# GpSimd forms the remaining parts of the weights of retention keys, retention values and pool input

## What is computed

```python
def hybrid_mixer(h, w_in, ...):
    proj = h @ w_in
    (dn_qkv, dn_z, dn_b, dn_a, ret_q, ret_k, ret_v, ret_g, pool_u, gates) = jnp.split(proj, ...)
    qkv = jax.nn.silu(causal_depthwise_conv(dn_qkv, dn_conv)).astype(f32)
    q, k, v = ...                       # l2_normalize of q and k
    beta, g = ...                       # from dn_b and dn_a
    o_dn = gated_delta_rule(q, k, v, beta, g)      # a triangular solve in chunks
    o_pool = multiscale_pool(pool_u, pool_w, pool_scale)
    o_ret = chunkwise_retention(rotary(ret_q), rotary(ret_k), ret_v, log_gamma)
    ...
def second_block(x, ...):
    for l in range(DEPTH):
        h = rms_norm_2(x, mix_pre_norm[l])
        x = x + rms_norm_2(hybrid_mixer(h, ...), mix_post_norm[l])
        h = rms_norm_2(x, ffn_pre_norm[l])
        x = x + rms_norm_2(swiglu(h, ...), ffn_post_norm[l])
```

## Time and profile before

| | |
|---|---|
| median of three runs | 1751.71 us |
| the profiled execution | 1752.36 us |
| its span in the trace | 1750.5 us |
| mean granted TensorE clock | 0.947 of full speed |

### The profile page before, as it was taken

The page is one execution under the profiler, slowest core; times in us unless marked ns, Lnnn a source line. Parts: engine busy times, 40 slices in busy tenths (PEclk is TensorE's granted clock), DMA queues, the critical chain, the costliest instruction groups (busy, mean ns, idle before and its releaser), DMA issues.

```text
span 1750.5 us, 18733 instructions
## 1 busy us (share of the span) xinstructions
PE 1587.8 (91%) x7866; PEld 1193.0 (68%) x7866; DVE 921.3 (53%) x1131; ACT 464.6 (27%) x621; POOL 44.9 (3%) x39
## 2 busy tenths in 40 slices
PE   6999999999998798799888799979879998979997
PEld 3755654565564496688744799859668874469986
DVE  2436652235754339865363666563876537266653
ACT  1121320031230144233201333333514330034332
POOL 0001000001000000000000000000000000000000
PEclk9999899999989898999999899989989999989999
DMA  7343122444212353243323365544414342245653
GB/s 263 121 145 120 48 97 81 160 144 134 83 68 82 122 169 121 80 137 121 127 97 122 119 185 177 195 148 152 136 49 145 121 151 96 68 142 176 192 176 113
DMA packets 140066, 226.75 MB, mean 130 GB/s; under 512 B 7968, under 2 KB 55376, under 8 KB 139856
## 3 DMA queue, kind: packets, MB, share of 16 engines
q1 hardware_dynamic: 133136, 221.60, 38.4%
q10 hardware_dynamic: 6848, 3.97, 0.8%
HBM read 224.50 MB, written 1.05 MB: 129 GB/s over the span
## 4 chain that ended last, share of the span: by engine, by line
PE 74%; DVE 18%; issue 3%; ACT 2%; POOL 1%; DMA 1%; ACTq 0%; POOLq 0%; DVEq 0%; SPq 0%
PE gp L475 19%; PE gp L458 19%; PE gp L487 17%; PE gp L529 6%; DVE arena L1055 5%; PE mp L714 4%; DVE arena L1094 3%; PE gp L451 3%; DVE wt_rest L1061 2%; DVE arena L1462 2%; POOL rs_out L1667 1%; PE mp L620 1%; PE mp L431 1%; DVE hT L1055 1%; DVE arena L1255 1%
## 5 line engine op out<-in xcount | busy, mean ns | idle before, releaser
L458 PE MATMUL gp<-wt,hT 128*128 128x512 f32 x512 | 227.9, 601 | 0.0
L458 PE MATMUL gp<-wt,arena 128*128 128x512 f32 x416 | 188.8, 614 | 22.2 <-DVE arena L1094 14.4
L475 PE MATMUL gp<-hT_hi,wt_hi 128*128 128x256 f32 x704 | 202.0, 287 | 6.9 <-DVE hT_rest L1061 6.9
L475 PE MATMUL gp<-hT_hi,wt_rest 128*128 128x256 f32 x704 | 201.6, 286 | 0.0
L475 PE MATMUL gp<-hT_rest,wt_hi 128*128 128x256 f32 x704 | 201.6, 286 | 0.0
L1061 DVE TENSOR_TENSOR wt_rest<-wt,mix_hi 128x1024 fp32r<-128x1024 f32 x120 | 141.5, 1221 | 95.4 <-ACT mix_hi L846 94.7
L1061 DVE TENSOR_TENSOR wt_rest<-wt,wt_hi 128x1024 fp32r<-128x1024 f32 x132 | 155.5, 1221 | 68.2 <-ACT wt_hi L846 68.2
L458 PEld LDWEIGHTS gp<-wt,hT 128*128 128x128 f32 x512 | 97.7, 194 | 113.9 <-issue 113.5
L458 PEld LDWEIGHTS gp<-wt,arena 128*128 128x128 f32 x416 | 81.6, 198 | 124.5 <-issue 113.5
L487 PE MATMUL gp<-mix_hi,mix_hT_hi 128*128 128x512 f32 x384 | 159.7, 416 | 7.2 <-DVE wt_rest L1061 7.2
L846 ACT ACTIVATE wt_hi<-wt 128x1024 fp32r<-128x1024 f32 x132 | 132.1, 1051 | 116.5 <-DMA wt<-in_ffn_down 59.0
(11 more groups left out here) (230 smaller groups left out, 2262.2 us busy)
## 6 DMA issues: line engine op xcount, KB each, us to landing
wt<-in_w_in SPq DMA_DIRECT2D x100, 1024.0 KB, 5.0
wt<-in_ffn_gate SPq DMA_DIRECT2D x44, 512.0 KB, 4.0
wt<-in_ffn_up SPq DMA_DIRECT2D x44, 512.0 KB, 5.0
wt<-in_w_out SPq DMA_DIRECT2D x20, 1024.0 KB, 5.0
wt<-in_ffn_down SPq DMA_DIRECT2D x20, 1024.0 KB, 5.0
wt<-in_w_mem_kv SPq DMA_DIRECT2D x8, 1024.0 KB, 10.4
wt<-in_w_branch_pool SPq DMA_DIRECT2D x4, 1024.0 KB, 5.3
wt<-in_w_branch_ret SPq DMA_DIRECT2D x4, 1024.0 KB, 6.4
```

The lines of the kernel that those rows point to most:

```text
L458: last = nc.tensor.matmul(group_bank(group, t), stationary(k0 + k, t), wt[:, u % SLOTS, k, :], start=(k0 + k == 0), stop=(k0 + k == GROUPS ...
L475: last = nc.tensor.matmul(o, a[:, k, P * c:P * c + P], b[:, :, k0 + k, :], start=(k0 + k == 0 and c % 2 == 0 and i == 0), stop=(k0 + k == ...
```

## The change

The subtractions of the parts of RK, RV and PU (twelve parts in each of the two layers) are issued on GpSimd instead of VectorE. They signal a semaphore of their own, `w_split_pool`, and TensorE waits for the one or the other by part. VectorE skips these parts in `weight_rests`. GpSimd first gives all powers that VectorE asks for up to the point behind unit 7 of the layer, then forms the layer's twelve parts in order, each when ScalarE has rounded it, and then goes on with the powers.

```diff
+POOL_GROUPS = {f"B{l}.{g}" for l in range(DEPTH) for g in ("RK", "RV", "PU")}
+POOL_PARTS = [n for n, (u, _, _) in enumerate(PARTS) if GROUPS[UNITS[u][0]][0] in POOL_GROUPS]
+VECTOR_PARTS = [n for n in range(len(PARTS)) if n not in POOL_PARTS]
...
-        w_rounded, w_split = sem("w_rounded"), sem("w_split")
+        w_rounded, w_split, w_split_pool = sem("w_rounded"), sem("w_split"), sem("w_split_pool")
...
+        pows_ahead_of_pool = {}
...
+        def split_by(n):
+
+            return (w_split_pool, POOL_PARTS.index(n) + 1) if n in POOL_PARTS else (w_split, VECTOR_PARTS.index(n) + 1)
...
-                pe.wait_ge(w_split, n + 1)
+                pe.wait_ge(*split_by(n))
...
             def weight_rests(count):
                 while halved[0] < count:
                     u, k, nk = PARTS[halved[0]]
+                    if halved[0] in POOL_PARTS:
+                        halved[0] += 1
+                        continue
...
                 rests_until(7)
-
+                pows_ahead_of_pool[l] = len(pow_widths)
...
         @block.gpsimd
         def _(pool):
-            for n, width in enumerate(pow_widths):
-                pool.wait_ge(pow_asked, n + 1)
-                nc.gpsimd.tensor_tensor(rs_out[:, 0:width], rs_in[:, 0:width], minus_half[:, 0:width], ALU.pow).then_inc(pow_given, 1)
+            def powers(first, end):
+                for n in range(first, end):
+                    pool.wait_ge(pow_asked, n + 1)
+                    width = pow_widths[n]
+                    nc.gpsimd.tensor_tensor(rs_out[:, 0:width], rs_in[:, 0:width], minus_half[:, 0:width], ALU.pow).then_inc(pow_given, 1)
+
+            done = 0
+            for l in range(DEPTH):
+                powers(done, pows_ahead_of_pool[l])
+                done = pows_ahead_of_pool[l]
+                for n in POOL_PARTS:
+                    u, k, nk = PARTS[n]
+                    if GROUPS[UNITS[u][0]][0][1] == str(l):
+                        pool.wait_ge(w_rounded, n + 1)
+                        nc.gpsimd.tensor_tensor(wt_rest[:, u % SLOTS, k:k + nk, :], wt[:, u % SLOTS, k:k + nk, :],
+                                                rounded_part(u)[:, k:k + nk, :].bitcast(F), ALU.subtract).then_inc(w_split_pool, 1)
+            powers(done, len(pow_widths))
```

## The result

The changed kernel takes 1759.22 us in the median of six runs (1756.94 to 1762.07), the kernel before 1753.33 us over its six. The ratio is 1.0039, with a 95% interval of 1.0024 to 1.0054: slower by 5.9 us as the medians have it, 4 to 9.5 us by the interval. The direction was forecast, but the forecast was 16 us slower, nearly three times what was measured. The profiled execution took 1760.49 us.

The account below looks back on a forecast made before the run. VectorE was taken to bound the one stretch touched in each layer. Removed pairs and collisions, -13.6 + 19.2 + 1.2 + 1.7 = +8.5 us a layer, +17 on 1752.4 us, gave about 1769, taken as 1768; range 1728 to 1776 us.

Parts of the forecast that it names:

- the pricing of the collisions: VectorE's chain, each layer: 19.2 us for RK's and RV's eight parts, 1.2 and 1.7 us for PU's.
- VectorE is the bound of the stretch: 656 to 730 us, once in each layer: VectorE busy 67.1 of 74 us, and TensorE's waits are nearly all for it.
- Exclusion: Chosen case, chance 0.50: VectorE and GpSimd shut each other out for whole instructions; +17 us, about 1768 us.
- independence: Rival, chance 0.27: the two engines do not disturb each other; 20 us faster, 1732 us.
- nothing of VectorE's own work leaves GpSimd an opening: Argued from VectorE's SBUF and PSUM copies: two-input work needs both SBUF streams, leaving none over for GpSimd; no separate size.
- A part takes 2.4 us on GpSimd: Twelve subtractions of 128x1024 a layer: estimated at 2.4 us each, between VectorE's 1.22 us and a power's 160 us.
- The slow rival: Rival, chance 0.07: twelve parts queued ahead of the 16-wide power delay it from 4 us a part; about 1800 us.
- Each of eight parts costs its whole length, 19.2 us: Three convolutions, each layer: RK's and RV's parts each hold VectorE for 2.4 us, 8 x 2.4 = 19.2 us.
- PU's parts cost 2.9 us: After the convolutions, each layer: 1.2 us charged on the products and the clamp, 1.7 us on the square.
- The sum: Each layer: -13.6 + 19.2 + 1.2 + 1.7 = +8.5 us; +17 us for two layers.
- Carried through at 99%: After the stretch TensorE's own work sets the pace at 99% busy, so a gain or loss in the stretch stays.

Follow-up runs that it names:

- the fills: Changed kernel with GpSimd filling the twelve parts of each layer with zeros instead of subtracting, reading nothing: 1728.26 us, ratio 0.9862.

## Why the prediction was right and wrong

The mechanism was right and its size was wrong. The step that failed is the pricing of the collisions: 19.2 + 2.9 us a layer were charged, and 17.3 and 18.9 us were paid. Since the sum is a small difference of two large terms, this halves it.

*VectorE is the bound of the stretch.* Right. Taking the subtractions away took 12.4 and 11.8 us off the chain for 13.6 us of pairs.

*Exclusion and not independence.* Right, and shown three ways: single instructions that end with GpSimd's, the write-only GpSimd instruction that leaves the multiply-adds alone, and the copies out of PSUM that never stretch. That nothing of VectorE's own work leaves GpSimd an opening, as the prediction argued from its copies, is too broad: in layer 0 a part that the square had held ran on from 705.63 to 707.91, and the sum that VectorE takes over SBUF meanwhile (`TENSOR_REDUCE`, one input) kept its 2.29 us. The rest agrees with the rule of the Trainium skill (SBUF — State Buffer, Who interferes with whom) that the forecast was weighed against, including its finer part, that an instruction with two SBUF inputs only collides with GpSimd's reads; the 5.06 us beside the fills is the number.

*A part takes 2.4 us on GpSimd.* Right: 2.37 to 2.55 us where no VectorE instruction held it. The slow rival is out. The power was not late, but in layer 0 only just: the last part ended at 707.91, and GpSimd then stood 0.33 us until the power began at 708.24.

*Each of eight parts costs its whole length, 19.2 us.* Too large by 2.4 us a layer. The first convolution lost 8.6 us to four parts (9.73 - 1.13), the other two 4.1 us each, 16.8 us together. Of each GpSimd instruction 0.25 us (beside scalings) to 0.4 us (beside multiply-adds) is not paid.

*PU's parts cost 2.9 us.* Too large in layer 0: 0.2 us on the clamp (0.88 instead of 0.69) and 0.3 us on the square (2.58 instead of 2.28), nothing on the products. The step took for granted that VectorE is always the one to wait. At the square it is the one that comes second, as single instructions of GpSimd and VectorE show, first in layer 0, then in layer 1:

```profile
703.44 4.47 POOL L1692 TENSOR_TENSOR wt_rest<-wt,mix_hi 128x1024 fp32r<-128x1024 f32 x1
703.05 2.58 DVE L1065 TENSOR_TENSOR arena<-arena 128x2048 f32<-128x2048 f32 x1
705.67 2.29 DVE L1503 TENSOR_REDUCE small<-arena 128x16 f32<-128x2048 f32 x1
...
1282.72 2.39 POOL L1692 TENSOR_TENSOR wt_rest<-wt,mix_hi 128x1024 fp32r<-128x1024 f32 x1
1283.08 4.18 DVE L1065 TENSOR_TENSOR arena<-arena 128x2048 f32<-128x2048 f32 x1
```

In layer 0 the square began 0.4 us ahead of the part, and the part took 2.1 us longer; in layer 1 the part began 0.4 us ahead, and the square took 1.9 us longer, where 1.7 were charged. Waiting of GpSimd costs nothing as long as TensorE does not yet want the part.

*The sum.* With the measured terms a layer gives -13.6 + 16.8 + 0.5 = +3.7 us in layer 0 and -13.6 + 16.8 + 0.2 + 1.9 = +5.3 us in layer 1, 9.0 us in all, instead of 17. The chain grew by 2.9 and 5.9 us, 8.9 in all; the 0.8 us less and more a layer are its waits for TensorE's transposes, which changed places (1.2 and 0.5 us before, 0.5 and 1.2 us after). So the terms account for the chain. The measured 5.9 us are less than 8.9, which lies inside the interval of 4 to 9.5 us. In the one profile of each kernel the lead-ins are 2.6 us shorter than before. As the same kernel shows such differences from one profile to the next, it stays open whether they belong to the change.

*Carried through at 99%.* Right on the whole. B took its two lengths in both kernels, before in the order 174.3 and 177.3, after in the order 176.9 and 174.7, and its sum did not change. The forecast left out that a stretch has two lengths 2.5 us apart, by the clock; here they cancelled, in the experiments they did not.

## What to carry to other kernels

Before moving elementwise work from VectorE to GpSimd, list what VectorE runs at the moment that the work comes up: beside copies out of PSUM it was free; beside one-input scalings from SBUF to SBUF and instructions with two SBUF inputs each GpSimd instruction cost VectorE most of its length, 2.05 to 2.15 us for a part that VectorE does in 1.13. One change with three parts can be a gain of 0.6 to 0.7% and two losses of 0.2 to 0.3% in one; run the parts alone. Where a sum is the difference of two large terms, an error of a fifth in one of them can halve it, as here. And look first for places in the slow engine's own queue where it stands still, since two pairs moved there gave about as much (0.9921) as the best move to the other engine (0.993 to 0.994), and both together gave 0.9880.

## What was not expected of the hardware

The order of waiting can turn: three products in a row held a GpSimd subtraction back for 2.7 us, while in the convolutions it was VectorE that waited at each collision. At the square the one that began first went through, but the part that came up inside the first product had to let the second and third pass as well; what decides there is not shown. A one-input scaling is held up by a GpSimd instruction that only writes (1.55 us for two fills), a two-input multiply-add is not. And TensorE's clock after the same waits came back at one of two times, worth some 2.5 us from one power to the next, in two layers of one execution.
